# A hybrid-attention encoder on one core: grid-attention items held four deep, normalised after the weighted sum, and returned to token order through HBM

## The reference, cut to what matters

```python
for l in range(DEPTH):                       # 2
    proj = rms_norm(x, g_mix[l]) @ w_in[l]
    o_a = dense_attention(qa, ka, va)        # kind A, 6 heads: all 1024 keys, plus 32 rotary features
    o_b = dilated_sliding_attention(...)     # kind B, 6 heads: bands, written as a table added to all 1024 scores
    o_c = neighbourhood_attention(...)       # kind C, 4 heads: the grid
    mixed = concat(rms_norm(o_a), rms_norm(o_b), rms_norm(o_c))
    x = x + mixed @ w_out[l]
    x = x + square(relu(rms_norm(x) @ w_mlp_in[l])) @ w_mlp_out[l]
return rms_norm(x, g_final)
```

## Time and profile before

| | |
|---|---|
| median of 3 runs | 2979.0 us (2977.97 to 2985.87) |
| the profiled execution's own time | 2986.88 us |
| its span, first to last instruction | 2985.1 us |
| attention stage, layer 0 / layer 1 | 286 to 670 us / 1759 to 2145 us |
| mean granted TensorE clock | 0.985 of 2.4 GHz |
| DMA, mean over the span | 94 GB/s |

### The profile page before, as it was taken

One profiled execution on the slowest core, in us unless ns is written; L12 is line 12 of the kernel. 1 busy time (PEld: TensorE's weight loads), 2 busy tenths in 40 slices (PEclk: granted clock), 3 DMA queues, 4 the chain that ended last, 5 costly groups with the idle time before them and its releaser, 6 DMA issues.

```text
span 2985.1 us, 39896 instructions
## 1 busy us (share of the span) xinstructions
PE 2872.7 (96%) x14640; PEld 2450.0 (82%) x14640; DVE 1753.1 (59%) x3038; ACT 1057.6 (35%) x1992; POOL 92.0 (3%) x69
## 2 busy tenths in 40 slices
PE   7999899998999999999998989999899999999998
PEld 7998778887888888888798977788788888888887
DVE  5642787885554555455666337878755555455457
ACT  5332666774311111111234235678732111111113
POOL 0000210000000000000000011200000000000000
PEclk9999999999999999999999999999999999999999
DMA  5656755413111111111146576543130111111111
GB/s 192 184 180 171 173 145 119 97 39 120 43 43 42 56 42 56 42 42 63 49 174 197 168 188 153 145 94 93 48 113 29 57 42 56 42 42 56 42 61 68
DMA packets 194007, 281.11 MB, mean 94 GB/s; under 512 B 47184, under 2 KB 153296, under 8 KB 184144
## 3 DMA queue, kind: packets, MB, share of 16 engines
q1 hardware_dynamic: 190032, 262.56, 30.6%
q0 software_dynamic: 3840, 16.78, 1.5%
HBM read 208.50 MB, written 70.78 MB: 94 GB/s over the span
## 4 chain that ended last, share of the span: by engine, by line
PE 82%; DVE 7%; issue 3%; DMA 3%; ACT 2%; DVEq 1%; SPq 1%; ACTq 0%; POOL 0%; POOLq 0%
PE ps L1356 23%; PE ps L1181 20%; PE ps L1371 18%; PE ps L1254 6%; PE ps L1271 5%; PE ps L1300 5%; PE ps L1311 2%; PE ps L1149 1%; DVE prob L1001 1%; DMA biasC<-in_bias_c 1%; PE ps L1218 1%; DVE x L1102 1%; DVE pT L831 1%; DMA values<-vst 1%; DVE hn L848 1%
## 5 line engine op out<-in xcount | busy, mean ns | idle before, releaser
L1371 PE MATMUL ps<-w_dn,hid 128*128 128x512 f32 x3072 | 712.9, 391 | 1.4
L1356 PE MATMUL ps<-hT,w_up 128*128 128x512 f32 x3072 | 702.5, 390 | 3.3 <-DVE hT L831 3.3
L1371 PEld LDWEIGHTS ps<-w_dn,hid 128*128 128x128 f32 x3072 | 573.8, 188 | 131.7 <-DVE x L1102 14.1
L1356 PEld LDWEIGHTS ps<-hT,w_up 128*128 128x128 f32 x3072 | 576.4, 188 | 122.9 <-ACT rbuf L781 3.7
L1181 PE MATMUL ps<-ws,hT 128*128 128x384 f32 (+3 forms) x3072 | 606.4, 356 | 2.7 <-issue 1.6
L1181 PEld LDWEIGHTS ps<-ws,hT 128*128 128x128 f32 x3072 | 535.6, 190 | 48.2 <-issue 2.4
L1102 DVE TENSOR_TENSOR x<-ps,x 128x512 f32<-128x512 f32 x512 | 342.7, 689 | 223.6 <-PE ps L1371 223.4
L718 ACT ACTIVATE pT<-ps 128x512 fp32r<-128x512 f32 (+1 forms) x448 | 240.6, 581 | 190.4 <-PE ps L1271 187.3
L1089 DVE TENSOR_TENSOR vbuf<-rbuf 128x512 f32<-128x512 f32 x128 | 88.6, 692 | 371.0 <-ACT rbuf L781 371.0
L831 DVE TENSOR_TENSOR pT<-ps,pT 128x512 fp32r<-128x512 f32 (+1 forms) x448 | 281.5, 664 | 13.8 <-ACT pT L718 13.8
L781 ACT ACTIVATE rbuf<-ps 128x512 f32<-128x512 f32 x128 | 76.6, 598 | 553.9 <-PE ps L1356 553.9
(11 more groups left out here) (84 smaller groups left out, 2142.8 us busy)
## 6 DMA issues: line engine op xcount, KB each, us to landing
raw<-in_wstream SPq DMA_DIRECT2D x76, 1024.0 KB, 4.9
head<-feats SPq DMA_DIRECT2D x192, 256.0 KB, 6.1
feats<-tst SPq DMA_DIRECT2D x128, 192.0 KB, 2.5
values<-vst POOLq DMA_DIRECT2D x32, 384.0 KB, 3.1
head<-values SPq DMA_DIRECT2D x24, 512.0 KB, 4.0
biasC<-in_bias_c SPq DMA_DIRECT2D x16, 768.0 KB, 7.7
raw<-in_wstream SPq DMA_DIRECT2D x12, 768.0 KB, 6.0
x_park<-x SPq DMA_DIRECT2D x16, 512.0 KB, 9.3
```

Source lines behind the costliest of these rows:

```text
L1356: last = pe.matmul(ps[:, k % 2, :], w_up[0 if first else 1][:, w1, kt, ft * P:(ft + 1) * P], hT[:, w2, kt, sh * 512:(sh + 1) * 512], start ...
L1371: last = pe.matmul(ps[:, 2 + m % 4, :], hid[slot][:, w1, ft, s * P:(s + 1) * P], w_dn[1 if last_group else 0][:, w2, ft, nh * 512:(nh + 1) ...
```

## The change

Four things change together; the diff below is cut to its core.

1. A grid item takes one PSUM bank of scores and half a row of `prob`, so that four are held at once; its transposes are done three steps after its scores instead of two (`TURN_STEP`), and its block's weighted sum begins one step later (`WEIGH_STEP`). For A and B items the steps are as before. So the two last transposes before an A head (items 15 and 16, say) fall into one step, and the step two after the first grid item has none.
2. The probabilities of grid items are no longer scaled before the transpose; the merged block is scaled, as for A and B. Each grid block is merged by itself, 4 matmuls.
3. The grid's result is not brought into token order by ACT. DVE writes it to `oC`, SP writes it from there to HBM with 8 DMAs (`park_grid`) and reads it back in token order one head later (`read_grid`, one DMA).
4. Neither queries nor bias are negated. POOL does nothing in this stage; L993 takes a maximum, and DVE negates it with one more `tensor_scalar` of 128 x 1.

```diff
+STEPS = NI + 12
+TURN_STEP = [n_ + (3 if kind_ == "C" else 2) for n_, (kind_, _, _) in enumerate(ITEMS)]
+WEIGH_STEP = [TURN_STEP[4 * b_ + 3] + 1 for b_ in range(NB)]
...
+def blocks_at(step):
+
+    return [b for b in range(NB) if WEIGH_STEP[b] + 3 == step]
...
+def slots(i):
+
+    return [2 * (i % 2) + i // 2 % 2] if ITEMS[i][0] == "C" else [2 * (i % 2), 2 * (i % 2) + 1]
...
+    grid_out = nc.dram_tensor("grid_out", [HC, SEQ, HD], f32).ap()
...
+    oC = [sb("oC0", [P, 8, HD], f32, "HN", 6 * KB), sb("oC1", [P, 8, HD], f32, "LAT", 7680)]
...
                 load_features(l, n)
+                if n >= 3 and HEADS[n - 3][0] == "C":
+                    read_grid(l, HEADS[n - 3][1] - HA - HB)
                 if kind == "C":
                     load_bias(l, 2 * (h - HA - HB))
                 load_values(l, n)
+                if n >= 2 and HEADS[n - 2][0] == "C":
+                    park_grid(l, n - 2)
                 if kind == "C":
                     load_bias(l, 2 * (h - HA - HB) + 1)
+
+            def park_grid(l, n):
+
+                k = HEADS[n][1] - HA - HB
+                sp.wait_ge(o_ready, l * NB + 2 * n + 2)
+                rows = grid_out[k].rearrange("(f r c) d -> f r c d", f=2, c=GRID_W)
+                for t in range(8):
+                    cb, hf = t // 2, t % 2
+                    sp.dma_start(rows[hf, :, 16 * cb:16 * cb + 16, :], oC[k % 2][:, t, :]).then_inc(grid_parked, 16)
+
+            def read_grid(l, k):
+
+                h = HA + HB + k
+                sp.wait_ge(grid_parked, (l * HC + k + 1) * 8 * 16)
+                sp.dma_start(O[:, :, h * HD:(h + 1) * HD], grid_out[k].rearrange("(t p) d -> p t d", p=P))\
+                  .then_inc(grid_back, 16)
...
-                for half in range(2 * HC):
-                    pool.wait_ge(biasc_in[half % 2], (l * HC + half // 2 + 1) * 16)
-                    hold(pool)
-                    bias = biasC[half % 2][:, :, :]
-                    pool.tensor_scalar(bias, bias, -1.0, None, ALU.mult).then_inc(biasc_neg, 1)
...
+                    for b in blocks_at(i):
                         act.wait_ge(pv_done, l * NB + b + 1)
...
+                        act.activation(oT[:, (b % 2) * 512:(b % 2 + 1) * 512], ps[:, 6 + b % 2, :], ACT.Copy)\
+                           .then_inc(ot_ready, 1)
...
+                            dve.wait_ge(biasc_in[n4 % 2], (l * HC + n4 // 2 + 1) * 16)
                             hold(dve)
+                            dve.tensor_tensor_reduce(out=score(i), in0=score(i), in1=biasC[n4 % 2][:, q % 4, :],
+                                                     scale=1.0, scalar=NEG, op0=ALU.add, op1=ALU.max,
+                                                     accum_out=a_mx[:, i:i + 1])
+                            dve.drain()
+                            dve.tensor_scalar(a_nm[:, i:i + 1], a_mx[:, i:i + 1], -1.0, None, ALU.mult)\
                                .then_inc(mx_ready, 1)
-                    if 1 <= i <= NI and ITEMS[i - 1][0] == "C":
-                        it = i - 1
-                        dve.wait_ge(p_ready, l * NI + it + 1)
-                        dve.reciprocal(a_rd[:, it:it + 1], a_den[:, it:it + 1])
-                        dve.drain()
-                        dve.tensor_scalar(prob[:, it % 2, 0:CW], prob[:, it % 2, 0:CW], a_rd[:, it:it + 1], None,
-                                          ALU.mult).then_inc(pn_ready, 1)
...
+                    for b in blocks_at(i - 3):
...
-                            dve.tensor_copy(O[:, :, cols],
-                                            ps[:, 6 + b % 2, :].rearrange("p (t d) -> p t d", d=HD))\
-                               .then_inc(o_ready, 1)
...
+                        dve.reciprocal(a_rd[:, 4 * b:4 * b + 4], a_den[:, 4 * b:4 * b + 4])
+                        dve.drain()
+                        dve.tensor_tensor(o, ps[:, 6 + b % 2, 0:4 * HD].rearrange("p (t d) -> p t d", d=HD),
+                                          a_rd[:, 4 * b:4 * b + 4].unsqueeze(2).to_broadcast([P, 4, HD]),
+                                          ALU.mult).then_inc(o_ready, 1)
...
+                for i in range(STEPS):
                     if i < NI:
                         scores(i)
...
+                    for it in turned_at(i):
+                        turns(it)
+                    for b in blocks_at(i - 2):
+                        merge(b)
+                    for b, part in weighed_at(i):
+                        weigh(b, part)
```

More of the change, by code:

```diff
@@ L89, with turned_at, weighed_at @@
 GRID_BEFORE = [sum(kind_ == "C" for kind_, _, _ in ITEMS[:n_]) for n_ in range(NI)]
+STEPS = NI + 12
+TURN_STEP = [n_ + (3 if kind_ == "C" else 2) for n_, (kind_, _, _) in enumerate(ITEMS)]
+WEIGH_STEP = [TURN_STEP[4 * b_ + 3] + 1 for b_ in range(NB)]
+def turned_at(step):
+    return [i for i in range(NI) if TURN_STEP[i] == step]
+def weighed_at(step):
+    return [(b, step - WEIGH_STEP[b]) for b in range(NB) if 0 <= step - WEIGH_STEP[b] < 4]
+def blocks_at(step):
+    return [b for b in range(NB) if WEIGH_STEP[b] + 3 == step]
+def slots(i):
+    return [2 * (i % 2) + i // 2 % 2] if ITEMS[i][0] == "C" else [2 * (i % 2), 2 * (i % 2) + 1]
+SLOT_BEFORE = [max([m_ for m_ in range(n_) if set(slots(m_)) & set(slots(n_))], default=-1) for n_ in range(NI)]
 GROUPS = []
@@ L235, in encoder @@
     eps = sb("eps", [P, 1], f32, "STAT", 192)
+    a_mx = sb("a_mx", [P, NI], f32, "STAT", 256)
     a_nm = sb("a_nm", [P, NI], f32, "STAT", 256 + 512)
@@ L732, in _ @@
                         use_table(ACT.Sqrt)
-                    if i >= 9 and (i - 9) % 4 == 0 and (i - 9) // 4 < NB:
-                        b = (i - 9) // 4
+                    for b in blocks_at(i):
                         act.wait_ge(pv_done, l * NB + b + 1)
[L736 to L751, removed]
+                        if b >= 2:
+                            act.wait_ge(mg_done, l * NB + b - 1)
+                        act.activation(oT[:, (b % 2) * 512:(b % 2 + 1) * 512], ps[:, 6 + b % 2, :], ACT.Copy)\
+                           .then_inc(ot_ready, 1)
+                act.wait_ge(o_ready, (l + 1) * NB)
+                act.wait_ge(grid_back, (l + 1) * HC * 16)
                 def output_weights(t):
@@ L1270, in turns @@
                             c = (4 * k + j) * P
-                            last = pe.transpose(ps[:, 4 + g % 2, j * P:(j + 1) * P], prob[:, i % 2, c:c + P],
+                            last = pe.transpose(ps[:, 4 + g % 2, j * P:(j + 1) * P], probability(i)[:, c:c + P],
                                                 ident[:, :])
@@ L1313, in merge @@
                     last.then_inc(mg_done, 1)
-                for i in range(NI + 12):
+                for i in range(STEPS):
                     if i < NI:
                         scores(i)
-                    if 2 <= i < NI + 2:
-                        turns(i - 2)
-                    if i >= 11 and (i - 11) % 4 == 0 and merged((i - 11) // 4):
-                        merge((i - 11) // 4)
-                    if i >= 6 and (i - 6) // 4 < NB:
-                        weigh((i - 6) // 4, (i - 6) % 4)
+                    for it in turned_at(i):
+                        turns(it)
[3 more added lines that the diff above has]
+                        weigh(b, part)
                 norm_turn(l, ST, 0)
@@ L1406 @@
 VALUE_N = [sum(VALUE_DMAS[kd] for kd, _ in HEADS[k::2]) for k in range(2)]
-MERGED = [ITEMS[4 * b][0] != "C" or b % 2 == 1 for b in range(NB)]
-NMG = sum(MERGED)
-def merged(b):
-    return b < NB and MERGED[b]
-def merges_before(b):
-    return sum(MERGED[:b])
 def turn_of(stg):
```

86 lines of the change are left out of this document (36 added, 50 removed).

## The result

The changed kernel takes 3050.1 us (median of 4 runs, 3047.0 to 3060.3) against 2982.4 us for the kernel before on the same chip: a ratio of 1.0236, 95% interval 1.0208 to 1.0265. It is slower, as forecast, but by 68 us instead of 22, and outside the stated range. The profiled execution of after has a span of 3058.5 us; that of before had 2985.1. The 73 us between these two are what has to be found; 10 of them are by how much the profiled execution of after (3060.3) lies above its median, and before's (2986.9) lies 4 above 2982.4.

What follows compares the result with a forecast made beforehand. Only a standing PE, 96% busy, or work added to it was taken to move the time. Grid heads 3, 5, 7 +37 and head 1 -15 gave +22 us on 2979: 3001 us, range 2974 to 3020.

Steps and rivals of the forecast that it cites:

- Gaps of 61 us in the grid heads, floor 14.7 to 14.8: Eight grid-head stretches: PE work without gaps takes 14.7 us before, 14.8 after; gaps total 61 us, the most to gain.
- POOL as their first cause: Grid heads: POOL negates each bias half in 4.31 us; DVE waits, and its scaling takes 3.60 us instead of 0.42.
- Parking in SP's queue: Grid heads 3, 5, 7: park_grid delays bias and features(n+1), making each stretch 27.0 us against 20.8.
- T + 24.8: Features' landing for the next A head, counted from a grid head's first scores (T); before, T + 15.2.
- +37: Sum for grid heads 3, 5 and 7 over both layers: +6.2 us, six times.
- 0.9 and 1.3: Added per grid head, us: 0.9 net for two transposes in one step when leaving it, 1.3 for the slower clock.
- The scores of four grid items in flight and the transpose one step later only add slack: Grid items in the attention stage: claimed that deeper holding and later transposes add only slack; no cost was given.
- The prediction's last sign: An idle PE in A or B heads would be something the prediction had not seen.
- The clock at 1.3 us a head: TensorE gets half its clock for a while after the long stall: 1.3 us taken, 0 least, 3.3 most.
- The stall for the bias falls inside that for the features: Grid heads 3, 5, 7: the second bias half is late, but its stall is hidden in the features' and not added.
- The rule on 256-byte writes: park_grid's writes to HBM are below the 512 B for line rate; by line rate alone nothing in the sum changes.
- The opposite rival: SP's queue has slack: features land by T + 14.8, stretches fall to 15.7 us, about -46, 2933 us; chance 0.13.

Runs made afterwards that it cites:

- e12: Changed kernel with parking behind features(n+1), all transposes two steps after scores, and the B heads' table loaded ahead of head 9: 2928.5 us, ratio 0.9825.
- e4: Kernel before, only without negating bias and queries (maximum and its negation on DVE, POOL idle in the attention stage): 2952.4 us, ratio 0.9902.
- e1: Changed kernel with park_grid moved behind features(n+1) in SP's queue and read_grid one head later: 2991.5 us, ratio 1.0037.
- e2: Changed kernel with grid transposes two steps after the scores instead of three, parking left in place: 3010.2 us, ratio 1.0085.
- e5: Changed kernel with parking behind features(n+1) and only the last two items of a grid head transposed two steps after scores: 2942.8 us, ratio 0.9874.
- e6: e3 with the exponential of the first two A items behind a grid head again waiting for a later transpose group: 2954.1 us, ratio 0.9922.
- e8: e2 with park_grid placed between the second bias half and features(n+1) in SP's queue: 2987.5 us, ratio 1.0015.
- e7: e2 with the 8 parking DMAs and their wait for o_ready issued by POOL's queue instead of SP's: 2942.5 us, ratio 0.9872.
- e3: Changed kernel with both parking behind features(n+1) and all transposes two steps after the scores: 2936.1 us, ratio 0.9849.
- e9: e3 without four-deep holding: each grid item has two banks and a whole row of prob, two in flight: 2938.6 us, ratio 0.9858.

## Why the prediction was wrong in size

- **Gaps of 61 us in the grid heads, floor 14.7 to 14.8**: right. e12 takes 54 of them away, with stretches of 15.3 to 15.7.
- **POOL as their first cause**: right, e4 shows it for 35 of the 61 us. One reading was not: the 2.55 us that PE stood at 372.94 were not for a long scaling. DVE's scaling there took 0.42 us; DVE had waited for the negated bias (first row below). Scalings of 2.8 to 3.8 us stand in the other seven grid heads, one in each, and the row of 3.60 us in the earlier trace rows is one of them. It began behind POOL's negation (second row) and ended 0.2 us after it.

```profile
371.74 0.57 DVE L993 CUSTOM_DVE_ANT_0 ps<-ps,biasC 128x384 f32<-128x384 f32 x1 [3.65 <-POOL biasC L556]
...
319.40 4.08 POOL L556 TENSOR_SCALAR biasC<-biasC 128x1536 f32<-128x1536 f32 x1 [4.89 <-DMA biasC<-in_bias_c]
```

  The Trainium skill, "SBUF — State Buffer", Who interferes with whom, has a rule for this: a DVE instruction in a 2-port mode, which a `tensor_scalar` can be, contends with GpSimd, and the one that comes first holds the shared ports for its whole instruction while the other blocks. The row agrees with it. No run here times the ports by themselves; in e4, without POOL's operation, every scaling took 0.42 us.
- **Parking in SP's queue**: the right mechanism, its size short. PE was to go on at T + 24.8 and went on at T + 27.4 on average: 24 us of the 39.6 that these six stretches lost. The forecast's +37 for them looks right only because 0.9 and 1.3, which belong behind the stretch, stood in it. The wait ended at T + 6.7 (6.45 predicted). The 8 issues took 5.0 to 5.1 us instead of 3.8, 0.64 each where 512-byte pieces took 0.47. From the bias issue to PE's start it was 15.7 us on average (15.0 to 16.5), where 14.5 had been taken to hold wherever it starts; in head 3 of layer 0, 3.7 MB were moved in it (223 GB/s over 16.46 us), and 3.1 MB in the 14.5 us of before (211 GB/s). Head 1 gained 17 us against 15, in part by luck: its stretches were 19.0 and 17.4 where 18.3 and 20.0 stood.
- **"The scores of four grid items in flight and the transpose one step later only add slack"**: this is the step that failed. I counted what a later transpose allows, and not who waits for it. Exp of an A item waits for the transposes of the items that held its row of `prob`; moving those from step i+2 to i+3 puts them behind another item's scores. Together with the step of two transposes, which I priced at 1.5 (its row at 399.21 shows 1.89) and netted to 0.9, the A stretches grew by 6.1 us on average, eight times: 48.7 us where 7 (and 10 for the clock) stood. By e1's stretch at the full clock some 3.0 of the 6.1 are waits, 24 us in all (an estimate); the rest goes with the clock. e2 and e5 take the cost away from two sides, e6 puts 2.3 us of it back by one wait. The prediction's last sign, an idle PE in the A heads, is what came.
- **The clock at 1.3 us a head**: too little. PEclk is 0.85 in the A stretches of 31 us. e1's two A stretches, 27.07 at 1.00 and 28.64 at 0.94, show 1.6 us for a fall of 0.06. From 27.07 to after's mean of 30.2 it is 3.1 us, 25 in all (an estimate), where 10 stood; before the change all eight A stretches ran at 1.00.
- **The stall for the bias falls inside that for the features**: right for the stall, wrong as a statement of what the bias costs there (e8).
- **The rule on 256-byte writes**: e7's stretches lie 1.4 us above the floor of 14.8, and no more of the writes' cost than that reached PE. The issue of one took 0.64 us against 0.47. The Trainium skill, "DMA: Bandwidth & Descriptors", Specifications, names 512 B as the least for line rate; its rule does not speak of the issue, and it would not have moved the forecast.
- **The opposite rival**, a queue with slack, gave 2933 us. e3 landed at 2936, but with the transposes moved back too; e1, with the queue alone relieved, came to 2991. The rival left out the cost of the later transposes as the forecast did, so that its number comes near e3's is no proof of its account.

## What to carry to other kernels

Before a step is moved later in an in-order pipeline, list everything that waits for it, and look at the seams where one kind of item follows another: there a buffer of one kind spans two of the other, and slack inside the run becomes a stall at its end. A DMA that waits for a late result belongs behind the loads in its queue, or in another queue. And when several edits come together, price each alone: here one edit carried most of the gain (e4), one carried none that shows (e9), and two placements turned a gain of 1.5% (e3) into a loss of 2.4%.

## What was not expected of the hardware

The same 10 feature DMAs landed 13.1 us after their first issue when the bias half had been issued 8.3 us ahead of them (e8), and 17.5 us after it when it had been issued 0.5 us ahead (e2). The 4.4 us between the two are near the 3.8 us that its 768 KB take at the 209 GB/s of e2's 17.5 us, which is an estimate:

```profile
366.47:383.99 17.52, 9.47 (x45) 8.04 (x44) 5.48 (x18) 4.75 (x13) 0.00 (x0) 0.73 1.01 209
```

And a stall cost more here than the time that PE stood. In after, grid stretches with waits of 4.8 to 6.1 and 2.4 to 2.9 us had 0.80 to 0.86 of the clock, and the A stretches behind them 0.85 to 0.95. The view by stretch, cut finer around 386.77 us, where an A stretch begins, shows where that comes from:

```profile
375.40:386.77 11.37, 4.98 (x20) 4.18 (x20) 5.30 (x18) 4.20 (x12) 0.00 (x0) 0.50 1.09 221
386.77:392.50 5.73, 5.73 (x17) 4.75 (x18) 2.23 (x4) 0.49 (x1) 0.00 (x0) 0.50 1.04 215
392.50:399.30 6.80, 3.97 (x24) 3.12 (x24) 3.56 (x4) 3.17 (x6) 0.00 (x0) 1.00 0.77 178
399.30:402.70 3.40, 3.40 (x13) 3.02 (x14) 1.01 (x2) 1.64 (x3) 0.00 (x0) 0.50 0.00 2
402.70:417.65 14.95, 14.95 (x99) 13.25 (x98) 12.08 (x17) 11.40 (x23) 0.00 (x0) 1.00 0.11 28
```

The clock fell to 1.2 GHz (0.50) while PE stood for the bias, and the first 5.7 us of the A stretch are still at that level: that is the grid head's stall. A second fall follows the A stretch's own waits of 0.94 and 1.89 us. In this stretch the first has the larger part, 5.7 us at the lower level against 3.4. The second does not always come: in e1 the A stretches of 27.07 us (1.00) and 28.64 us (0.94) have the same waits ahead and inside (1.7, 0.9 and 1.9 us).
